# Layer 0's experts in blocks of 32 rows in four column groups, with rows moved two blocks at a time through rings of four

## The reference, cut to what matters

```python
def moe_ffn(h, router_w, router_b, w_gate, w_up, w_down):
    probs = jax.nn.softmax((h @ router_w).astype(jnp.float32), axis=-1)
    ...   # a group of experts is chosen, and the 2 best of it; weights in combine
    for e in range(N_EXPERTS):
        y_e = (jax.nn.silu(h @ w_gate[e]) * (h @ w_up[e])) @ w_down[e]
        out = out + combine[:, e:e + 1] * y_e
```

## Time and profile before

| | us |
|---|---|
| median of 3 runs | 1832.29 (1827.73 to 1833.35) |
| profiled execution, its own time | 1833.7 |
| its span in the trace | 1832.0 |
| PE busy | 1678.9 (92%) |
| DVE, ACT, POOL busy | 712.1, 412.6, 293.1 |

### The profile page before, as it was taken

The page is one execution under the profiler, slowest core; times in us unless marked ns, Lnnn a source line. Parts: engine busy times, 40 slices in busy tenths (PEclk is TensorE's granted clock), DMA queues, the critical chain, the costliest instruction groups (busy, mean ns, idle before and its releaser), DMA issues.

```text
span 1832.0 us, 29176 instructions
## 1 busy us (share of the span) xinstructions
PE 1678.9 (92%) x11470; PEld 1020.5 (56%) x11470; DVE 712.1 (39%) x1586; ACT 412.6 (23%) x866; POOL 293.1 (16%) x263
## 2 busy tenths in 40 slices
PE   5999998989999999799999988999789999899975
PEld 2467554554444444355656555676547888456543
DVE  3578863650110111511111157688665111433222
ACT  4011212551000001322222250111035100333321
POOL 0004342870000000200000020044356000000000
PEclk9999997999999999999999988998799999999998
DMA  9410469319222152489999834115581346599995
GB/s 392 136 47 24 155 259 288 81 69 337 100 95 89 69 217 110 182 317 386 384 394 383 326 120 115 47 37 192 203 190 47 140 159 253 230 369 398 410 410 228
DMA packets 107341, 384.16 MB, mean 210 GB/s; under 512 B 40992, under 2 KB 60704, under 8 KB 68064
## 3 DMA queue, kind: packets, MB, share of 16 engines
q1 hardware_dynamic: 85360, 335.44, 49.1%
q0 software_dynamic: 4272, 30.67, 4.9%
q10 hardware_dynamic: 17600, 16.49, 3.1%
HBM read 363.18 MB, written 31.98 MB: 216 GB/s over the span
## 4 chain that ended last, share of the span: by engine, by line
PE 70%; DVE 8%; DMA 8%; POOL 5%; issue 3%; SPq 3%; ACT 2%; ACTq 0%; POOLq 0%; DVEq 0%
PE tile_ps L639 59%; PE turn_ps L639 4%; PE out_ps L639 4%; DMA arena<-sorted_in 4%; POOL arena L2052 3%; SPq L556 3%; DMA vn<-in_wpack 1%; PE turn_ps L964 1%; DVE arena L1916 1%; DMA x<-in_xT 1%; DMA ring<-in_wpack 1%; DVE smx L1898 1%; ACT arena L1396 1%; PE tile_ps L858 0%; ACT h L1174 0%
## 5 line engine op out<-in xcount | busy, mean ns | idle before, releaser
L639 PE MATMUL tile_ps<-h,ring 128*128 128x512 f32 (+1 forms) x1312 | 477.3, 519 | 4.1 <-ACT h L1174 3.7
L639 PEld LDWEIGHTS tile_ps<-h,ring 128*128 128x128 f32 x1312 | 254.2, 195 | 210.7 <-issue 193.8
L639 PE MATMUL tile_ps<-arena,ring 128*128 128x512 f32 (+1 forms) x704 | 235.3, 486 | 2.7 <-issue 2.7
L639 PE MATMUL tile_ps<-arena 128*32 128x256 f32 (+3 forms) x2096 | 210.2, 393 | 21.8 <-DVE arena L1716 4.9
L639 PEld LDWEIGHTS tile_ps<-arena,ring 128*128 128x128 f32 x704 | 133.6, 190 | 96.6 <-issue 87.6
L639 PEld LDWEIGHTS tile_ps<-arena 128*32 128x32 f32 (+2 forms) x2096 | 125.3, 130 | 68.7 <-issue 41.3
L2052 POOL TENSOR_SCALAR arena<-arena,smx 128x512 f32<-128x512 f32 (+1 forms) x96 | 128.9, 1360 | 70.1 <-DVE smx L1904 69.8
L1369 ACT ACTIVATE arena<-tile_ps 128x512 f32<-128x512 f32 (+1 forms) x56 | 27.4, 490 | 347.3 <-PE tile_ps L639 347.3
L1937 DVE TENSOR_TENSOR arena<-tile_ps,arena 128x512 f32<-128x512 f32 (+1 forms) x32 | 17.9, 559 | 212.1 <-PE tile_ps L639 212.1
L639 PE MATMUL out_ps<-arena 64*128 64x64 f32 (+1 forms) x968 | 83.8, 330 | 10.2 <-issue 10.2
L639 PE MATMUL tile_ps<-h,arena 128*32 128x256 f32 (+1 forms) x336 | 80.4, 482 | 4.8 <-ACT arena L1396 4.8
(11 more groups left out here) (328 smaller groups left out, 2288.1 us busy)
## 6 DMA issues: line engine op xcount, KB each, us to landing
ring<-in_wpack SPq DMA_DIRECT2D x176, 1024.0 KB, 8.6
arena<-in_wpack SPq DMA_DIRECT2D x64, 1024.0 KB, 16.0
h<-in_wpack SPq DMA_DIRECT2D x15, 1024.0 KB, 19.3
qa<-in_wpack SPq DMA_DIRECT2D x12, 1024.0 KB, 15.8
qn<-in_wpack SPq DMA_DIRECT2D x12, 1024.0 KB, 17.8
kn<-in_wpack SPq DMA_DIRECT2D x12, 1024.0 KB, 19.8
vn<-in_wpack SPq DMA_DIRECT2D x12, 1024.0 KB, 22.6
sorted_out<-arena ACTq DMA_DIRECT2D x44, 128.0 KB, 8.0
```

Source lines behind the costliest of these rows:

```text
L639: return nc.tensor.matmul(out, lhsT, rhs, start=start, stop=stop)
```

## The change

Layer 0 now takes 32 rows a block (`bs = BS1`), 39 blocks for the counts above: in the order in which the experts are taken, 3, 2, 2, 2, 3, 4, 2, 2, 4, 2, 2, 3, 2, 2, 3, 1 (the order itself follows the sizes, and so changes a little).

- A block's 1024 channels lie as four groups of 32 partitions by 256 columns in `hrow`; two transposes of 128 by 128 turn them. `gate_up` has 32 products of 32 rows with 128 columns for each half, in four column groups (up, up, gate, gate); `down` has 8 of 32 rows with 256 columns for each half, in four column groups.
- `turn_hidden(0)` stands ahead of the last two steps of gate and up of half 1; the wait for DVE's product of half 0 stands at the third step from the end. All of `turn_rows` stands ahead of the last down half.
- Rows come in two blocks at a time into a ring of four blocks, `row_ring` (32 partitions), and DVE copies a block from there to `hrow` with four copies of 32 by 256, addressed by a register. Results go to a ring of four blocks, `y_ring`: ACT copies two column groups of them, DVE the other two. POOL stores two blocks at a time; ACT starts no DMAs in the loop.
- Four blocks instead of two are picked by products at the start (128 rows as before); ACT copies the last two of them into `row_ring`, and PE waits for that ahead of its loop.
- `sorted_in` and `sorted_out` have 1792 rows instead of 2048, and the transfers that fill them early are that much smaller; `ht` lies elsewhere in the arena.

```diff
@@ -58,9 +58,10 @@
 BS = 64
 BS1 = 32
-ROWS_OF = [BS, BS1]
-MAXBLK = 32
-GU_STEPS, DOWN_STEPS = [4, 1], [2, 1]
+MAXBLK = 48
+SORTED = 1792
+RINGED = 4
+GU_STEPS = [2, 1]
...
+                def pick_rows(r):
+                    pe.wait_ge(hot_done, r // 2 + 1)
+                    marks = (hot, hot_next)[r // 2][:, :, r % 2 * BS1:(r % 2 + 1) * BS1]
+                    for n in range(len(tiles)):
+                        for q in range(4):
+                            ins = mm(first_bank[r][group(q)], marks[:, n, :], ht[:, n, q * 256:(q + 1) * 256],
+                                     n == 0, n == len(tiles) - 1)
+                    ins.then_inc(first_full, 1)
+                def turn_rows(r):
+                    pe.wait_ge(hrow_ready[l], r + 1)
+                    for h2 in range(2):
+                        ins = nc.tensor.transpose(rows_bank[:, h2 * P:(h2 + 1) * P], hrow[:, h2 * P:(h2 + 1) * P],
+                                                  c("ident"))
+                    ins.then_inc(turned_in[l], 1)
...
                 def turn_hidden(half):
-                    for f in (0, 1):
-                        ins = nc.tensor.transpose(hid_bank[half][:, f * BS:(f + 1) * BS],
-                                                  hid[:, (2 * half + f) * P:(2 * half + f + 1) * P],
-                                                  c("ident")[0:BS, 0:BS])
-                    ins.then_inc(turned_hid[l], 1)
+                    nc.tensor.transpose(hid_bank[half], hid[:, half], c("ident")[0:2 * BS1, 0:2 * BS1])\
+                        .then_inc(turned_hid[l], 1)
...
-                def gate_up(e, r, half):
+                def gate_up(e, r, half, ks):
                     wg, wu = (arrived(e, half * 2 + n) for n in range(2))
-                    for k in range(KD):
-                        if half == 1 and k == KD - 1:
-                            pe.wait_ge(hrow_ready[l], r * 2 + 2)
-                        g = mm(gu_bank[half][BS:P], hsT[:, k], wg[:, k], k == 0, k == KD - 1)
-                        if half == 1 and k == KD - 1:
-                            pe.wait_ge(hid_done[l], r * 2 + 1)
-                        u = mm(gu_bank[half][0:BS], hsT[:, k], wu[:, k], k == 0, k == KD - 1)
-                    g.then_inc(gu_full[l], 1)
-                    u.then_inc(gu_full[l], 1)
+                    for k in ks:
+                        for q, w in enumerate((wu, wu, wg, wg)):
+                            if (half, k, q) == (1, KD - 3, 3):
+                                pe.wait_ge(hid_done[l], r * 2 + 1)
+                            ins = mm(gu_bank[half][group(q)], hsT[:, k % 2, group(k // 2)],
+                                     w[:, k, q % 2 * P:(q % 2 + 1) * P], k == 0, k == KD - 1)
+                    return ins
...
                     for f in range(2):
-                        for n in range(2):
-                            if (half, f, n) == (0, 1, 1):
+                        for n in range(4):
+                            if (half, f, n) == (0, 1, 3):
                                 pe.wait_ge(hid_done[l], r * 2 + 2)
-                            ins = mm(y_bank[n * BS:(n + 1) * BS], hidT[:, 2 * half + f],
-                                     wd[:, f, n * 512:(n + 1) * 512], half + f == 0, half + f == 2)
-                            if half + f == 2:
-                                ins.then_inc(down_full[l], 1)
...
+                            ins = mm(y_bank[group(n)], hidT[:, half, group(f)], wd[:, f, n * 256:(n + 1) * 256],
+                                     half + f == 0, half + f == 2)
+                    return ins
+                pick_rows(0)
+                pick_rows(1)
+                turn_rows(0)
+                pick_rows(2)
+                pick_rows(3)
+                pe.wait_ge(ring_in, RINGED)
                 now = 0
                 for e in range(NEXP):
                     after = before(pe, e + 1)
                     with pe.Fori(now, after) as r:
                         pe.wait_ge(hsT_done[l], r + 1)
-                        gate_up(e, r, 0)
-                        gate_up(e, r, 1)
+                        gate_up(e, r, 0, range(KD)).then_inc(gu_full[l], 1)
+                        gate_up(e, r, 1, range(KD - 2))
                         turn_hidden(0)
-                        turn_rows(range(4))
+                        gate_up(e, r, 1, range(KD - 2, KD)).then_inc(gu_full[l], 1)
                         pe.wait_ge(y_taken[l], r + 1)
+                        pe.wait_ge(y_other, r + 1)
                         down(e, r, 0)
                         turn_hidden(1)
-                        turn_rows(range(4, KD)).then_inc(turned_in[l], 1)
-                        down(e, r, 1)
+                        turn_rows(r + 1)
+                        down(e, r, 1).then_inc(down_full[l], 1)
...
+                for r in (2, 3):
+                    act.wait_ge(first_full, r + 1)
+                    for q in range(4):
+                        ins = nc.scalar.copy(row_ring[:, r - 2, q * 256:(q + 1) * 256],
+                                             first_bank[r][q * BS1:(q + 1) * BS1])
+                ins.then_inc(ring_in, RINGED)
                 act.wait_ge(route_done, l + 1)
-                act.wait_ge(filled, 32)
                 with act.Fori(0, before(act, NEXP)) as r:
                     for half in range(2):
-                        act.wait_ge(gu_full[l], r * 4 + (2 * half + 2))
-                        A(hid[:, half * 256:(half + 1) * 256], gu_bank[half][BS:P], ACT.Silu).then_inc(sg_done[l], 1)
-                    for half in range(2):
+                        act.wait_ge(gu_full[l], r * 2 + (half + 1))
+                        A(hid[:, half], gu_bank[half][2 * BS1:P], ACT.Silu).then_inc(sg_done[l], 1)
                         act.wait_ge(turned_hid[l], r * 2 + (half + 1))
-                        nc.scalar.copy(hidT[:, 2 * half:2 * half + 2].rearrange("p k n -> p (k n)"), hid_bank[half])\
-                            .then_inc(hidT_done[l], 1)
-                    act.wait_ge(rows_out[l], r * 32 + 32)
-                    act.wait_ge(down_full[l], r * 2 + 2)
-                    nc.scalar.copy(ysb, y_bank).then_inc(y_taken[l], 1)
-                    act.wait_ge(y_taken[l], r + 2)
+                        nc.scalar.copy(hidT[:, half], hid_bank[half]).then_inc(hidT_done[l], 1)
+                    act.wait_ge(ring_out, r + 1)
+                    act.wait_ge(down_full[l], r + 1)
                     for n in range(2):
-                        act.dma_start(sorted_out[bass.ds(r * BS, BS)][:, n * 512:(n + 1) * 512],
-                                      ysb[n * BS:(n + 1) * BS]).then_inc(rows_out[l], 16)
+                        ins = nc.scalar.copy(y_ring[:, bass.ds(r % RINGED, 1), n * 256:(n + 1) * 256].rearrange("p a n -> p (a n)"),
+                                             y_bank[n * BS1:(n + 1) * BS1])
+                    ins.then_inc(y_taken[l], 1)
...
-                def copy_rows_in(r):
+                def turned(r):
                     dve.wait_ge(turned_in[l], r + 1)
-                    CP(hsT.rearrange("p k n -> p (k n)"), rows_bank).then_inc(hsT_done[l], 1)
-                dve.wait_ge(first_full, 2 * l + 1)
-                CP(hrow[:, 0:512], first_bank[0][0:BS]).then_inc(first_done, 1)
-                copy_rows_in(0)
-                dve.wait_ge(first_full, 2 * l + 2)
-                CP(hrow[:, 0:512], first_bank[1][0:BS]).then_inc(hrow_ready[l], 1)
+                    CP(hsT.rearrange("p a n -> p (a n)"), rows_bank).then_inc(hsT_done[l], 1)
+                dve.wait_ge(first_full, 1)
+                CP(hrow, first_bank[0]).then_inc(hrow_ready[l], 1)
+                turned(0)
+                dve.wait_ge(first_full, 2)
+                CP(hrow, first_bank[1]).then_inc(hrow_ready[l], 1)
                 with dve.Fori(0, before(dve, NEXP)) as r:
                     for half in range(2):
                         dve.wait_ge(sg_done[l], r * 2 + (half + 1))
-                        v = hid[:, half * 256:(half + 1) * 256]
-                        TT(v, gu_bank[half][0:BS], v, ALU.mult).then_inc(hid_done[l], 1)
-                    copy_rows_in(r + 1)
+                        TT(hid[:, half], gu_bank[half][0:2 * BS1], hid[:, half], ALU.mult).then_inc(hid_done[l], 1)
+                    turned(r + 1)
+                    dve.wait_ge(ring_in, r + 3)
+                    for q in range(4):
+                        ins = CP(hrow[q * BS1:(q + 1) * BS1],
+                                 row_ring[:, bass.ds(r % RINGED, 1), q * 256:(q + 1) * 256].rearrange("p a n -> p (a n)"))
+                    ins.then_inc(hrow_ready[l], 1)
+                    dve.wait_ge(ring_out, r + 1)
+                    dve.wait_ge(down_full[l], r + 1)
+                    for n in range(2, 4):
+                        ins = CP(y_ring[:, bass.ds(r % RINGED, 1), n * 256:(n + 1) * 256].rearrange("p a n -> p (a n)"),
```

(37 more changed lines are left out.)

67 lines of the change are left out of this document (27 added, 40 removed).

## The result

The changed kernel takes 1841.19 us (median of 10 runs, 1836.86 to 1855.75) against 1826.50 for the kernel before (10 runs on the same chip, 1816.02 to 1833.79): a ratio of 1.0081 with a 95% interval of 1.0055 to 1.0106. It is slower by 0.8%, and the forecast of 1822 was wrong in sign; 1841 also lies above its range. The profiled execution took 1840.06 us with a span of 1838.1.

The account below looks back on a forecast made before the run. The prediction took PE's block chain as the bound, with weight loads close behind. Blocks of 6.6 us end the stage 19.6 us earlier; 9.6 given back leaves 10.0, so 1822 us on the median, range 1811 to 1838.

Parts of the forecast that it names:

- 27 ns a record: PE's gate and up products: 128 records a block at 27 ns each, 3.45 us (2.7 to 6.9).
- Rival 5: Slower through PE's issue: 54 ns an issue rate, a block 10.1 us, time about 1947; chance 0.03.
- Sum 3.45 + 1.73 + 0.85 + 0.4 + 0.2 = 6.6 us a block: PE's block: gate and up, down, pause between down halves, pause for half 0's turn, wait for half 0; 5.8 to 7.4.
- Pause between the down halves: PE between the down halves: one narrow and two wide transposes, smaller ACT copy; 0.85 us (0.7 to 1.0), before 0.93.
- wait for half 0's product: PE waiting in each block for DVE's product of half 0, held up by ACT: 0.2 us (0 to 0.5).
- forecast gain of 19.6: End of PE's blocks in the stage: at 1031 instead of 1050.6, before anything is given back.
- Weights and PE level: Stage end: last weights land at 1026.7, their products end at 1028, PE alone at 1027, together 1031; chance 0.56.
- The start: First block of the stage: PE waits for ACT's copies of the last picked block, starting about 0.9 us later, at 770.0.
- What is given back: Behind the last block: later copies 1.4, last store 5.7, gathers 2, warm-up 0.5; together 9.6 us lost.
- The row load leaves the path: PE's chain between blocks: rows are asked for about four blocks ahead, so their load no longer delays PE.
- Rival 4: Slower through ACT's loop back to PE: product ready at 4.1 us, block 7.5, time 1846; chance 0.14.
- Rival 3: No measurable change: a block of 6.85 to 7.2 us, time 1827 to 1837; chance 0.15.

Follow-up runs that it names:

- e5: Changed kernel with one PE stop a block instead of two (all gate and up products, then all turns, then all down products): 1829.49 us, ratio 1.0029 to before.
- e3: Changed kernel with PE's order changed: next rows' turns right behind the last gate and up product, half 1's turns after four down products: 1850.04 us, ratio 1.0125 to before.
- e1: Changed kernel loading only 256 of 2048 columns of each weight slot of layer 0's experts 3 to 15 (output wrong): 1828.85 us, one run.
- e6: Changed kernel loading 1024 of 2048 columns of each weight slot of layer 0's experts 3 to 15 (output wrong): 1842.12 us, one run.
- e9: Changed kernel loading 16 of 128 partitions, all 2048 columns, of each weight slot of layer 0's experts 3 to 15 (output wrong): 1831.68 us, one run.
- e10: e5 with only 256 of 2048 columns of the weights of layer 0's experts 3 to 15 (output wrong): 1814.77 us, one run.
- e7: e4 with one PE stop a block, all turns between the up and the down products: 1823.57 us, ratio 0.9974 to before.
- e2: Kernel before, loading only 256 of 2048 columns of each weight slot of layer 0's experts 3 to 15 (output wrong): 1823.85 us, one run.
- e4: Kernel before, 64-row blocks kept, rows loaded a block ahead into free partitions and moved up by DVE: 1816.97 us, ratio 0.9956 to before.

## Why the prediction was wrong

1. **Products.** "27 ns a record" and 54 ns for the down halves: right (1.31 us for 48 records). Rival 5 is out.
2. **"Sum 3.45 + 1.73 + 0.85 + 0.4 + 0.2 = 6.6 us a block": this is the step that failed.** It measured 7.12. The term that was mis-sized is "Pause between the down halves [...] 0.85 (0.7 to 1.0)": it measured 1.25, since half 1's hidden product comes 0.31 us too late in every block, a wait that the prediction has no term for. The other terms are close: products 5.21 for 5.18, `turn_hidden(0)` and the wait for half 0's product together 0.67 for 0.6. So 0.40 of the 0.52 us are this one pause. 39 x 0.52 = 20 us, the whole forecast gain of 19.6. e5 is the test: with the stops put together the block is 6.60.
3. **Stalls.** No term: 7.4 us in the profiled execution, up to 11.6 in e3. The block alone takes the gain away (e1, with 7.12 us a block and no stalls, took 1828.85 in its one run); that the loss comes from the stalls fits this, and is argued rather than shown. More instructions in less time is the change itself (15932 matmul records in the run instead of 11470, 20 instruction packets in the stage instead of 12). In the six 32-row traces that have them there are 28 stalls over 0.4 us, and all 28 lie in the first block behind a border, many in the same block in several versions (the longest stall of the changed kernel, of e5, e6 and e9 is in the eighth block each time). Two things happen there at once: PE runs a loop's code for the first time, and SP issues the weights that the ended expert makes room for. With the second made small the stalls go in e1, though not in e9 and e10. Runtime: NRT & Kernel Launch of the Trainium skill (Instruction fetch mechanics) says that instructions are fetched in blocks of 16 KiB while the current ones run, that this is mostly hidden, and that a taken branch to a place outside the fetched window breaks it. The size of the packets and the first pass agree with the trace; "mostly hidden" holds before and not after. Whether a branch plays a part no run here shows.
4. **"Weights and PE level":** weights were never reached; the DMA share fell to 0.73, and PE waited for no weights. With PE 26 us slower than forecast the weights' 1028 did not matter. The number itself was not far off: e7, the one version whose PE was fast enough, ran into the weights at a stretch of 273.
5. **The start:** 767.47 for a forecast of 770.0; but this point lay between 761.2 and 780.2 in all these profiles, so it says nothing.
6. **What is given back.** "A transfer of rows beside weights takes 8.0 us": the last store took 3.53, because the stage ended later than the loads for layer 1. Of 9.6 us given back 1.25 for the store can be read, and the gathers took 6.13 where they had taken 6.37.
7. **The row load leaves the path:** right, and worth 8 to 9 us of the stage (e2, e4). It is the part of the change that gains.
8. **Rivals.** Rival 4 gave 7.5 us a block and 1846; the stretch divided by 39 is 7.49 and the time 1841, but not by its mechanism: half 0's product comes too late by 0.29 only. Rival 3 named the right danger ("six short waits in a block") and a block of 6.85 to 7.2, where the block is, but has no stalls.

Why the blocks of 32 could not win here: 7.12 us for 32 rows against 12.39 for 64 (e4) is 57%. With 39 small blocks for 22 large ones, 39 x 7.12 = 278 against 22 x 12.39 = 273, even with every row wait gone. At e5's 6.60 it would be 257, but e5 gave that back in stalls and low clock.

## What to carry to other kernels

Smaller blocks save streaming in proportion and pay the fixed part of a block in full. Before halving a block, divide one of its passes, from start to start, into records times rate and the rest; here the rest was 1.9 us of 7.1, and the break-even was 12.8 x 22 / 39 = 7.2. Where a change joins two ideas (narrow blocks, rows fetched ahead), price and try each alone: here one cost more than the other gained. And when an engine has to run many more instructions in the same time, look for idle time of kind "issue" in the middle of a run of products.
